# A mixture-of-experts kernel on one Trainium2 core: the last expert's rows are added by a one-hot product instead of a store and a gather

## The reference, cut to what matters

```python
logits = jnp.dot(xf, w_router, ...) + b_router
vals, idx = lax.top_k(logits, TOP_K)
gate = jax.nn.softmax(vals, axis=-1)
...
up = jnp.dot(xb, w_up[eb]) + b_up[eb]
glu, lin = jnp.split(up, 2, axis=-1)
glu = jnp.minimum(glu, SWIGLU_LIMIT)
lin = jnp.clip(lin, -SWIGLU_LIMIT, SWIGLU_LIMIT)
act = glu * jax.nn.sigmoid(SWIGLU_ALPHA * glu) * (lin + 1.0)
yb = jnp.dot(act, w_down[eb]) + b_down[eb]
out = jnp.zeros((N + 1, D_), h.dtype).at[row_tok].add(yb * row_gate[:, None])
```

## Time and profile before

| | |
|---|---|
| median of 3 runs | 1860.7 us (1860.04 to 1865.69) |
| the profiled execution's own time | 1861.18 us |
| its span | 1859.4 us |
| PE busy | 1740.1 us, 94% of the span |
| DVE, ACT, POOL busy | 555.9, 415.5, 106.4 us |
| DMA | 545.45 MB, mean 293 GB/s |
| granted TensorE clock, mean | 0.972 |

### The profile page before, as it was taken

How to read it: one execution, slowest core, us unless ns; L and a number is a source line. 1 busy time by engine, 2 the same in 40 slices (tenths; PEclk the granted TensorE clock), 3 DMA queues, 4 the chain that set the end, 5 groups by cost and what they waited for, 6 DMA issues and landing times. The chain is left out here.

```text
span 1859.4 us, 39736 instructions
## 1 busy us (share of the span) xinstructions
PE 1740.1 (94%) x17331; PEld 1017.3 (55%) x17331; DVE 555.9 (30%) x770; ACT 415.5 (22%) x692; POOL 106.4 (6%) x121
## 2 busy tenths in 40 slices
PE   6999998999999999999999999999859798799888
PEld 4875652343434434343443434344449787698888
DVE  2273172121111112111111211111346551676754
ACT  2344152000000000000000000000034266355442
POOL 0111020000000000000000000000000044110000
PEclk9999989999999999999999999999979899899999
DMA  9987395999999999999999999999616243333452
GB/s 344 345 286 244 133 338 210 388 396 407 401 397 399 399 398 395 400 398 393 392 403 404 394 399 397 399 398 408 226 51 196 63 135 93 113 116 112 136 148 80
DMA packets 187878, 545.45 MB, mean 293 GB/s; under 512 B 16216, under 2 KB 90216, under 8 KB 154952
## 3 DMA queue, kind: packets, MB, share of 16 engines
q1 hardware_dynamic: 172432, 519.49, 74.0%
q10 hardware_dynamic: 10968, 15.40, 2.3%
q0 software_dynamic: 4416, 9.69, 1.6%
HBM read 526.06 MB, written 17.84 MB: 293 GB/s over the span
## 5 line engine op out<-in xcount | busy, mean ns | idle before, releaser
L1428 PE MATMUL ps<-ring_low,xg 128*32 128x512 f32 x3072 | 344.6, 597 | 0.0
L1428 PE MATMUL ps<-first_ring,xg 128*32 128x512 f32 x3072 | 335.4, 592 | 0.0
L1559 DVE TENSOR_SCALAR gl<-ps 128x768 f32<-128x768 f32 x32 | 30.6, 957 | 684.1 <-PE ps L1428 684.1
L1428 PEld LDWEIGHTS ps<-first_ring,xg 128*32 128x32 f32 x3072 | 99.5, 110 | 230.1 <-issue 230.1
L1428 PEld LDWEIGHTS ps<-ring_low,xg 128*32 128x32 f32 x3072 | 96.4, 110 | 206.6 <-issue 200.8
L1451 PE MATMUL ps<-first_ring,aT 128*32 128x256 f32 x3072 | 173.3, 382 | 2.3 <-ACT aT L1510 2.3
L1451 PE MATMUL ps<-raw_more,aT 128*32 128x256 f32 x3072 | 171.6, 379 | 0.0
L1451 PEld LDWEIGHTS ps<-first_ring,aT 128*32 128x32 f32 x3072 | 100.4, 111 | 82.5 <-issue 20.2
L1504 ACT ACTIVATE sg<-gl 128x768 f32<-128x768 f32 x32 | 27.0, 844 | 510.8 <-DVE gl L1559 510.8
L1451 PEld LDWEIGHTS ps<-raw_more,aT 128*32 128x32 f32 x3072 | 99.9, 110 | 65.9
L1662 DVE TENSOR_TENSOR low<-ring_low,high 128x2048 fp32r<-128x2048 f32 x42 | 98.7, 2350 | 121.5 <-ACT high L1655 121.0
(11 more groups left out here) (487 smaller groups left out, 1879.6 us busy)
## 6 DMA issues: line engine op xcount, KB each, us to landing
first_ring<-in_w_up_dram SPq DMA_DIRECT2D x128, 1024.0 KB, 6.6
ring_low<-in_w_up_dram SPq DMA_DIRECT2D x128, 1024.0 KB, 6.3
raw_more<-in_w_down_dram SPq DMA_DIRECT2D x64, 1024.0 KB, 6.7
first_ring<-in_w_down_dram SPq DMA_DIRECT2D x64, 1024.0 KB, 6.7
ring_low<-in_w_in_dram SPq DMA_DIRECT2D x39, 1024.0 KB, 5.3
first_ring<-in_w_ada_dram SPq DMA_DIRECT2D x7, 2048.0 KB, 20.3
ring_low<-in_w_ada_dram SPq DMA_DIRECT2D x5, 2048.0 KB, 18.2
y_dram<-ye ACTq DMA_DIRECT2D x32, 288.0 KB, 5.7
```

Source lines behind the costliest of these rows:

```text
L1428: mm = pe.matmul(ps[32 * q:32 * q + 32, u, :], xg[:, k, 32 * block_of:32 * block_of + 32], w[:, :, 256 * f:256 * f + 256], start=False, st ...
L1559: dve.tensor_scalar(gl[:], ps[:, 0:3, 0:256], LIMIT, None, ALU.min).then_inc(s(tag, "glu_ready"), 1)
```

## The change

- The store of expert 31 (`store("", NE - 1, ...)`) is gone, and GpSimd fetches place 0 as soon as experts 0 to 30 are stored, behind place 1. The rows of expert 31 in `y_dram` then hold something else, so the gate of place 0 is set to 0 for a token that expert 31 serves (`gate0`).
- In the routing block, VectorE also makes `last_row` (a token's row number within expert 31), `last_gate` and `gate0`; all three and `first_row` now live in the tile `rstd`. The product of totals (line 1165) has 128 result rows instead of 1.
- At the start of the expert block, VectorE makes for each token tile a one-hot row that holds the gate in the column of the token's row (`li`, line 1633 of the changed kernel), TensorE turns these by eight products with the identity (1492, 1494) ahead of the up products of expert 0, and VectorE copies them to `picks` (96 rows) and `picks3` (the three pieces of 32 rows, in partitions 96 to 127 of the tile that also holds `bdn`).
- At the end, TensorE makes the bias products of banks 0 to 2 between `turn` and the down products of expert 31, that of bank 3 behind them, and then adds `picks` and `picks3` times `ye` to the same banks (`last_rows`). VectorE's order is now: places 3, 2 and 1, the copy to `ye`, place 0, and the banks per tile.
- ScalarE makes one Sqrt of a single column behind its last copy to `aT`.

```diff
@@ -1037,12 +1037,15 @@
         gate4 = sb("gate4", [P, TT, TOPK], at=moe)
-        bdn = sb("bdn", [NE, D], at=moe)
+        low_high = sb("low_high", [P, D], at=moe)
+        bdn = low_high[0:NE, :]
+        last_row, last_gate, gate0 = [rstd[:, TT * i:TT * i + TT] for i in range(3)]
         xsel = sb("xsel", [P, KT, TOTAL + ROWS], at=moe)
         flag = sb("flag", [1, 1], I32, at=moe)
-        first_row = sb("first_row", [1, PER * (NE + 1)], I32, at=moe)
+        first_row = rstd[0:1, 32:32 + PER * (NE + 1)].bitcast(I32)
...
@@ -1162,9 +1165,8 @@
                         .then_inc(sm("places_summed"), 1)
-                    pe.matmul(ps[0:1, 7, 0:NE], cst[:, C_ONES:C_ONES + 1], sel[:, 0, :], start=True, stop=False)
-                    pe.matmul(ps[0:1, 7, 0:NE], cst[:, C_ONES:C_ONES + 1], sel[:, 1, :], start=False, stop=True)\
-                        .then_inc(sm("totals_summed"), 1)
+                    pe.matmul(ps[:, 7, 0:NE], ones, sel[:, 0, :], start=True, stop=False)
+                    pe.matmul(ps[:, 7, 0:NE], ones, sel[:, 1, :], start=False, stop=True).then_inc(sm("totals_summed"), 1)
                     mod(17, 4)
...
@@ -1246,7 +1248,6 @@
                     V.link(dve, dve.memset(lg[:, :, NE:], -2e38))
-                    V.link(dve, dve.memset(first_row[:], 0))
                     for i in range(TOTAL // P):
...
@@ -1309,10 +1310,15 @@
                     V.link(dve, dve.tensor_single_scalar(flag[:], fl, float(ROWS), ALU.is_gt))
+                    V.link(dve, dve.memset(first_row, 0))
                     for r in range(PER):
                     V.link(dve, dve.memset(xsel[:, :, TOTAL:], 0.0))
+                    V.link(dve, dve.tensor_scalar(last_row, place[:, :, NE - 1], ps[:, 7, NE - 1:NE], float(-TOTAL - 1),
+                                                  ALU.add, ALU.add))
+                    V.link(dve, dve.tensor_copy(last_gate, gate[:, :, NE - 1]))
                     V.link(dve, dve.tensor_copy(dest[:], place4[:, :, 0:TOPK]))
...
@@ -1321,6 +1327,8 @@
                                                   mine.rearrange("p t j e -> p (t j) e"), AX.X, ALU.add))
+                    V.link(dve, dve.scalar_tensor_tensor(gate0, last_row, 0.0, gate4[:, :, 0], ALU.is_lt, ALU.mult))
                     rest(2, NE)
...
@@ -1340,6 +1348,10 @@
         diag = gl[:, 0, :].rearrange("p (t n) -> p t n", t=TT)
+        picks = sb("picks", [ROWS, TT * P], at=moe)
+        picks3 = low_high[ROWS:P, 0:3 * TT * P].rearrange("p (u n) -> p u n", u=3)
         sq = xsel[:].rearrange("p k r -> p (k r)")[:, 0:KT * SEQ].rearrange("p (k t) -> p k t", k=KT)
...
@@ -1400,7 +1412,7 @@
                 for j in PLACES:
-                    pool.wait_ge(s("", "ye_stored"), 32 * (NE - j))
+                    pool.wait_ge(s("", "ye_stored"), 32 * (NE - max(j, 1)))
                     if j == 0:
...
@@ -1453,14 +1465,34 @@
-                def down_bias(tag):
+                def down_bias(banks, last):
+                    for b in banks:
+                        t, h = divmod(b, 2)
+                        mm = pe.matmul(ps[:, b, :], gT[:, t * P:(t + 1) * P], bdn[:, 512 * h:512 * h + 512],
+                                       start=True, stop=last, skip_group_check=not last)
+                    return mm
+                def last_rows():
                     for t in range(TT):
-                        for h in range(2):
-                            mm = pe.matmul(ps[:, 2 * t + h, :], gT[:, t * P:(t + 1) * P], bdn[:, 512 * h:512 * h + 512],
-                                           start=True, stop=True)
-                    mm.then_inc(s(tag, "bias_summed"), 1)
+                        at = slice(t * P, (t + 1) * P)
+                        pe.matmul(ps[:, 2 * t, :], picks[:, at], ye[0:ROWS, 0:2, :].rearrange("p u n -> p (u n)"),
+                                  start=False, stop=True, skip_group_check=True)
+                        pe.matmul(ps[:, 2 * t + 1, 0:256], picks[:, at], ye[0:ROWS, 2, :], start=False, stop=True,
+                                  skip_group_check=True)
+                        for u in range(3):
+                            mm = pe.matmul(ps[:, 2 * t + 1, 256:512], picks3[:, u, at], ye[ROWS:P, u, :], start=False,
+                                           stop=(u == 2), skip_group_check=True)
+                        mm.then_inc(s("", "bias_summed"), 1)
+                pe.wait_ge(sm("hot31_ready"), TT)
+                for t in range(TT):
+                    at = slice(256 + t * P, 256 + (t + 1) * P)
+                    pe.matmul(ps[0:ROWS, 5, at], li[:, t, 0:ROWS], idn, start=True, stop=True)
+                    for u in range(3):
+                        mm = pe.matmul(ps[ROWS:P, 5 + u, at], li[:, t, 32 * u:32 * u + 32], idn, start=True, stop=True)
+                mm.then_inc(sm("hot31_turned"), 1)
                 up("", 0)
...
@@ -1468,18 +1500,22 @@
                 turn("", NE - 1)
+                pe.wait_ge(sm("bdn_in"), 16)
+                down_bias(range(3), False)
                 down("", NE - 1)
-                pe.wait_ge(sm("bdn_in"), 16)
-                down_bias("")
+                down_bias(range(3, 4), False).then_inc(s("", "bias_started"), 1)
+                pe.wait_ge(s("", "bias_started"), 1)
+                pe.wait_ge(s("", "ye_copied"), NE + 1)
+                last_rows()
                 with flagged(pe):
-                    pe.wait_ge(s("", "added"), TT * TOPK)
+                    pe.wait_ge(s("", "bias_added"), TT)
                     with pe.Fori(0, NE) as e:
                             down("more_", n)
-                    down_bias("more_")
+                    down_bias(range(4), True).then_inc(s("more_", "bias_summed"), 1)
                 pe.wait_ge(sm("diag_ready"), TT)
...
@@ -1528,8 +1564,11 @@
                 turned("", NE - 1)
-                store("", NE - 1, 0, NE - 1)
+                act.activation(sg[:, 0, 0:1], cst[:, C_ONES:C_ONES + 1], ACT.Sqrt).then_inc(s("", "sig_ready"), 1)
                 with flagged(act):
+                    act.wait_ge(s("", "xg_ready"), 2 * (NE + 1))
+                    act.wait_ge(s("", "sig_ready"), NE + 1)
                     rows("more_", 0, 0)
...
@@ -1539,8 +1578,9 @@
                     act.wait_ge(s("more_", "added"), TT * TOPK)
+                    act.wait_ge(s("more_", "xg_ready"), 2 * (NE * PER + 1))
                 for t in range(TT):
-                    act.wait_ge(s("", "added"), TT * (TOPK - 1) + t + 1)
+                    act.wait_ge(s("", "bias_added"), t + 1)
                     S.done(act, act.activation(sq[:, 4 * t:4 * t + 4, :].rearrange("p k t -> p (k t)"), acc[:, t, :], ACT.Square,
...
@@ -1572,21 +1612,29 @@
                         dve.wait_ge(s(tag, f"got{j}{t}"), 16)
+                        weight = gate0[:, t:t + 1] if j == 0 and not tag else gate4[:, t, j:j + 1]
                         if j == PLACES[0]:
-                            ins = dve.tensor_scalar(acc[:, t, :], got[:, t, BUFFER[j], :], gate4[:, t, j:j + 1], None, ALU.mult)
+                            ins = dve.tensor_scalar(acc[:, t, :], got[:, t, BUFFER[j], :], weight, None, ALU.mult)
                         else:
                             dve.wait_ge(s(tag, "added"), TT * PLACES.index(j) - TT + t + 1)
-                            ins = dve.scalar_tensor_tensor(acc[:, t, :], got[:, t, BUFFER[j], :], gate4[:, t, j:j + 1],
+                            ins = dve.scalar_tensor_tensor(acc[:, t, :], got[:, t, BUFFER[j], :], weight,
                                                            acc[:, t, :], ALU.mult, ALU.add)
                 def add_bias(tag):
-                    dve.wait_ge(s(tag, "bias_summed"), 1)
                     for t in range(TT):
-                        dve.wait_ge(s(tag, "added"), TT * (TOPK - 1) - TT + t + 1)
+                        dve.wait_ge(s(tag, "bias_summed"), 1 if tag else t + 1)
+                        dve.wait_ge(s(tag, "added"), TT * (TOPK - 1 if tag else TOPK) - TT + t + 1)
                         dve.tensor_tensor(acc[:, t, :], acc[:, t, :], bank2(2 * t), ALU.add).then_inc(s(tag, "bias_added"), 1)
+                for t in range(TT):
+                    V.done(dve, dve.tensor_scalar(li[:, t, 0:ROWS], cst[:, C_IOTA:C_IOTA + ROWS], last_row[:, t:t + 1],
+                                                  last_gate[:, t:t + 1], ALU.is_equal, ALU.mult), sm("hot31_ready"))
+                dve.wait_ge(sm("hot31_turned"), 1)
+                V.link(dve, dve.tensor_copy(picks[:], ps[0:ROWS, 5, 256:512]))
+                V.link(dve, dve.tensor_copy(picks3, ps[ROWS:P, 5:8, 256:512]))
                 dve.memset(ye[:], 0.0).then_inc(s("", "ye_copied"), 1)
...
@@ -1597,13 +1645,12 @@
                 add("", 2)
+                add("", 1)
                 dve.wait_ge(s("", "ye_stored"), (NE - 1) * 32)
                 copy_y("", NE - 1)
-                add("", 1)
+                add("", 0)
                 add_bias("")
-                add("", 0)
```

(2 more changed lines are left out.)

3 lines of the change are left out of this document (1 added, 2 removed).

## The result

| | before | after |
|---|---|---|
| median, same chip, 19 runs each | 1864.48 us (1860.01 to 1866.09) | 1868.79 us (1860.68 to 1873.66) |
| the profiled execution's own time | 1861.18 us | 1869.44 us |
| its span | 1859.4 us | 1867.7 us |
| granted TensorE clock, mean | 0.972 | 0.966 |

The ratio is 1.0023, with a 95% interval of 1.0012 to 1.0034: about 4.3 us slower. The forecast was 1860.3 us, no change, with a range up to 1864.5; the measured median lies above it. Of the distance of 8.5 us 3.8 lie in the base: the forecast started from 1860.7 us, the median of three runs, and the kernel before has 1864.48 here. The forecast step was -0.35 us, the measured one +4.3, and 1860.7 + 4.3 = 1865.0 lies above the range too. The changed kernel's executions spread over 13.0 us, the kernel before's over 6.1; the one that was profiled took 1869.44 us, near the median.

A forecast was written before the change was run, and what follows sets the result against it. TensorE, busy throughout the expert loop, was taken as the bound, so only the expert stage's start and end count: +1.5 - 1.85 = -0.35 us on 1861.18, 1860.3 us against the three-run median; range 1855.2 to 1864.5.

The forecast's parts named there:

- (a): Expert block's end: three bias banks ahead of the last down keep full clock, no 1.7 us loss; down ends about 1340.3.
- (b): VectorE's copy to ye waits for place 1's fetch, landing at 1342.7; ye is ready 2.0 us later than before.
- (c): Last expert's products on TensorE: 5.75 us plus 1.7 us of lost clock, 7.45 us; bounds 5.5 and 11.5.
- rival B: Expert block's end: fetch lands late, clock stays down; 1864.0 us, or 1868.2 all at half clock; chance 0.15, harder form 0.05.
- (d): Behind the last products: one bias add and two hand-overs; last square at 1354.0 instead of 1355.85, 1.85 us won.
- (e): ScalarE's dummy Sqrt: the table load stays between mean and root, 0 gained; off the path, 1.3 us.
- (f): Expert stage's start: added routing operations and eight turning products start expert 0's up 1.5 us later; bounds 0.8 to 2.5.
- A: Expert block's end: place 1's fetch doesn't hold the copy; 6.75 us won, 5.25 net, 1855.4 us; chance 0.15.
- C: Last expert's products: 32-row ones run beside 96-row ones, some 1.6 us go, 1858.7 us; chance 0.15.
- D: ScalarE's table load does leave the path before the root, 1859.0 us; chance 0.05.

The follow-up runs named there:

- warm_fill: The changed kernel with four unread full-array products of 512 columns in TensorE's wait for ye; 1863.54 us, ratio 1.0007.
- loads_late: The changed kernel with SyncE's three 1 MB loads for the second block waiting until place 0's fetch has landed; 1859.05 us, ratio 0.9977.
- copy_first: The changed kernel with VectorE's copy of the last expert's rows to ye ahead of the adds of place 1; 1860.92 us, ratio 0.9989.
- cold_own: The changed kernel with TensorE waiting for all adds of places 3 to 0 before the last expert's products; one run, 1872.76 us.
- cold_full: As cold_own, but the ten products take all 128 rows (identity and the whole of ye, other sums); one run, 1867.97 us.
- best: The changed kernel with copy_first and start_late, three routing operations later, first_row's memset back in idle time, Sqrt behind the flagged branch; 1856.44 us, ratio 0.9968.
- before_both: The kernel before with only three bias banks ahead of the last down and a dummy Sqrt behind the flagged branch; 1860.53 us, ratio 0.9996.
- start_late: The changed kernel with the eight turning products behind the up products of expert 0 instead of ahead; 1865.83 us, ratio 1.0018.
- thin_fill: The changed kernel with warm_fill's four filling products, but over 32 rows of the array instead of 128; one run, 1873.76 us.
- full_shape: The changed kernel with its ten products over 128 rows (identity and the whole of ye, other sums), wait unchanged; one run, 1860.06 us.
- best_fill: best with unread full-array products: six of 256 columns at the routing's end, six of 512 ahead of the diag product; 1855.07 us, ratio 0.9959.
- final: best and loads_late together, with four unread full-array products of 512 columns ahead of the diag product; 1854.71 us, ratio 0.9946.

## Why the prediction was wrong

**(a) The bias banks and the clock: right.** The first down half took 5.39 us (7.07 before). After the start's 2.76 us are taken off, down ends where it was said to (1342.9 - 2.76 = 1340.2; said 1340.3). Of the thirteen kernels with this order twelve took 5.39 us there; warm_fill's profiled execution took 7.07, with PE busy throughout and the clock down to 0.50 from 1334 to 1336. So the six 32-row records that fill the gap hold the clock mostly, not surely.

**(b) The copy held by the fetch: right.** Said was a landing at 1342.7, with the start's shift 1345.5; it was 1345.93, 8.5 us behind its issue instead of 7.9. Products start at 1348.23 where 1345.1 plus 2.76 gives 1347.9. The wait was PE's wait for VectorE, and VectorE's for the DMA. loads_late shows its cause, which the prediction left open: the second block's loads.

**(c) The products: the step that failed.** The terms of shape were right: copy_first's 6.0 us at full clock stand beside the 5.75 worked out. The clock term was mis-sized: "I charge the same 1.7 us of lost clock" took the price of the gap of (a). There what followed the gap were products over 128 rows and four column groups, which brought the clock back; here it was products over 96 and 32 rows, which did not. The term is 11.5 us, the upper bound, and 4.0 more than the 7.45 taken: the lost clock costs 5.5 us where 1.7 were charged. cold_own and cold_full differ in the shape of the ten products (and in the values they multiply), and their 11.5 and 7.5 us are the two sizes. The bound "all at half clock" was named, but had a chance of 0.05 only, in rival B's harder form. Of the 4.45 us between the forecast step (-0.35) and the 4.1 us of the traces, 4.0 are this term.

**(d) What stands behind: right.** The last square is one add and two hand-overs behind the products. By its own sum it should have started at 1354.0; without the start's shift it is 1361.11 - 2.76 = 1358.35. The miss of 4.35 is 4.0 from (c) and the rest, 0.35, from (b). So 1.85 won became 2.5 lost.

**(e) The early root: right.** The load stayed between mean and root, as the order listing had it. best and before_both show that it leaves the path when the dummy Sqrt stands behind the branch instead of ahead of it. The page "ScalarE: Activation LUTs" of the Trainium skill (What ACT_TABLE_LOAD costs) adds a drain of 1380 ns to the load; here the root follows the load's end by 0.01 us (1362.62 + 1.28 to 1363.91), and no drain is seen.

**(f) The start: somewhat low in its sum, wrong inside.** 1.5 us were said, with bounds of 0.8 and 2.5. From the mark in the routing to the last transposes the seven other kernels with the start as changed took 1063.5 to 1064.6 us, the changed one 1063.9, the two with the old start 1062.1 and 1060.7: 1.8 more in the profiled pair, 2.7 by the means, which is over the upper bound. Inside, `up` started 2.6 us later behind that mark and not 1.5, since it could start only 3.2 us behind the first turning product and not 2.25 (the last turning record ended 4.3 us behind it): "the half clock that lies over 290 to 292 is paid before as after" was wrong in both directions. The turning products ran under it wholly (clock 0.50 up to 294), and `up` got 0.8 us of it back (1037.5 to 1036.7 from its start to the transposes). Of the routing's operations about 0.2 us went on to VectorE, as said: the block's first VectorE operation is at 288.79 instead of 287.66, and 0.9 of these 1.13 us lie ahead of the routing's mark. On ScalarE it was 0.4: in start_late, with the turning out of the way, `up` starts 25.0 us behind the mark where it was 24.6 before.

**The rivals.** A, a fetch that doesn't hold the copy, is what copy_first and loads_late make of the kernel: in loads_late the last square starts 22.8 us behind the last transpose, 6.3 less than before, where A's sum had 6.75. B in its harder form is what happened, at its 11.5 us and with a fetch 0.6 us later than foreseen rather than 4. That its 1868.2 stands near the measured 1868.79 is chance: it is 7.5 us above the forecast's base, and the measured step is 4.3. C fell: at full clock the 96-row and the 32-row products took 6.0 us one behind the other, where C wanted 1.6 less. The rule of the page "TensorE: Matmul & The Clock Gate" of the Trainium skill (Part 3: Packing small matmuls), that matmuls in different row groups run concurrently, isn't borne out for a 96-row product beside 32-row ones, though the 64-row products of the earlier trace rows do overlap. D fell as said.

**What stays open.** PE's stops under "issue" of 0.3 to 2.4 us at the end of expert 31 (thin_fill, full_shape, best_fill, final) have no releaser in the profile; the DMA queues were full in each (share 1.0 to 1.1), but they were in the changed kernel too, which has no such stop there (1.10 from 1338 to 1340), and the cause was not looked for by a run. The second block took 480.1 to 481.1 us in five of the fourteen traces and 482.8 to 484.0 in the other nine; why is not known. Which executions of the changed kernel are its fast ones (down to 1860.68 us), and whether the fetches land sooner in them, isn't shown: one was profiled. cold_own, cold_full, thin_fill and full_shape are one execution each, and cold_full's weights are the identity in place of the one-hot rows; a run that changes the values alone was not made.

## What to carry to other kernels

Before work is moved to TensorE to save a round trip through memory, ask how full of the array it is and at what clock it will run: ten products worth 6 us cost 11.5 behind a wait of 4 us, and the remedy was to remove the wait (copy first, or hold back the loads that delay the fetch) and not to shorten the products. Charge a gap on TensorE by what follows it, not by what the last gap cost. And look at what an engine's queue holds ahead of the one copy that the new path hangs on: one line moved on VectorE won some 6 us by the ratios, more than the change had lost.

## What the runs showed of the hardware

- A busy TensorE was not enough for the full clock here: with products over 96 and 32 rows and no idle time the granted clock stayed at 0.50 for 11.5 us (cold_own), and under a 32-row filler it fell from 1.00 to 0.50 (thin_fill); with products over 128 rows it was back about 4 us after their start (cold_full). It need not fall at once: behind full work the same thin products kept 1.00 for 6.0 us (copy_first, warm_fill).
- With three loads of 1 MB in flight on SyncE's queue the indirect fetches on GpSimd's landed 6.8 to 9.4 us behind their issue, without them 4.2 to 6.3 (the changed kernel against loads_late).
- Ahead of the flagged branch the early Sqrt was lost: a table load stood at the join and one more, of 1.28 us, ahead of the root. Behind the join it took these 1.28 us off the path (best, before_both).
